# A causal mask added by VectorE in PSUM for short attention jobs, by a TensorE matmul for long ones

## What is computed

```
def masked_softmax(s, mask):
    sf = jnp.where(mask, s.astype(jnp.float32), NEG)      # NEG = -1e30
    m = jnp.max(sf, axis=-1, keepdims=True)
    e = jnp.where(mask, jnp.exp(sf - m), 0.0)
    p = e / jnp.maximum(jnp.sum(e, axis=-1, keepdims=True), TINY)
    return p.astype(s.dtype)
...
s = jnp.einsum('bgrqd,bgkd->bgrqk', qb, kb) * scale       # NSA, causal
s = jnp.einsum('bhqd,bhkd->bhqk', qb, k) * scale          # MLA, causal
...
x = x + merged @ w_out[l]
x = x + jnp.square(jax.nn.relu(hn @ w_up[l])) @ w_down[l]
```

## Time and profile before

| | |
|---|---|
| median of 3 runs | 1598.51 us (1595.76 to 1598.61) |
| profiled execution, its own time | 1601.22 us |
| span of its profile | 1599.4 us |
| granted TensorE clock, mean | 0.989 of full speed |
| PE busy | 1539.1 us, 96% |
| DVE / ACT / POOL busy | 892.5 / 722.9 / 423.1 us |

### The profile page before, as it was taken

One profiled execution on the slowest core, in us unless ns is written; L12 is line 12 of the kernel. 1 busy time (PEld: TensorE's weight loads), 2 busy tenths in 40 slices (PEclk: granted clock), 3 DMA queues, 4 the chain that ended last, 5 costly groups with the idle time before them and its releaser, 6 DMA issues.

```text
span 1599.4 us, 23215 instructions
## 1 busy us (share of the span) xinstructions
PE 1539.1 (96%) x7566; PEld 1269.8 (79%) x7566; DVE 892.5 (56%) x1354; ACT 722.9 (45%) x1315; POOL 423.1 (26%) x442
## 2 busy tenths in 40 slices
PE   6999999899999999999999999999999999999996
PEld 4888788777888888888888777877778888888885
DVE  5765655566754453535566655555575535454455
ACT  5753666774432222222466546767634322222232
POOL 0301566567010010101011025756740201010010
PEclk9999999999999999999999999999999999999998
DMA  4243221114422322322323412211243222323223
GB/s 181 86 145 126 73 68 67 39 67 139 138 93 94 101 95 92 105 92 94 105 80 119 159 65 61 72 67 41 86 165 106 92 93 95 102 92 104 93 92 106
DMA packets 43526, 155.55 MB, mean 97 GB/s; under 512 B 5312, under 2 KB 5312, under 8 KB 43424
## 3 DMA queue, kind: packets, MB, share of 16 engines
q1 hardware_dynamic: 37440, 134.23, 25.3%
q0 software_dynamic: 5408, 17.95, 3.1%
q10 hardware_dynamic: 576, 2.10, 0.3%
HBM read 143.78 MB, written 10.49 MB: 96 GB/s over the span
## 4 chain that ended last, share of the span: by engine, by line
PE 79%; DVE 6%; issue 6%; ACT 5%; POOL 2%; DMA 1%; ACTq 0%; DVEq 0%; POOLq 0%
PE G L1337 13%; PE G L1339 13%; PE G L1338 13%; PE O L1337 8%; PE O L1338 8%; PE O L1339 8%; PE O L1603 3%; PE T L1579 2%; PE S L1562 2%; POOL wsplit L472 2%; PE T L1337 1%; DVE nmx L1103 1%; PE T L1339 1%; PE T L1338 1%; PE O L1412 1%
## 5 line engine op out<-in xcount | busy, mean ns | idle before, releaser
L569 ACT ACTIVATE wsplit<-stage 128x1024 fp32r<-128x1024 f32 x230 | 243.5, 1059 | 617.9 <-PE G L1339 283.4
L891 DVE TENSOR_TENSOR wsplit<-stage,wsplit 128x1024 fp32r<-128x1024 f32 x184 | 266.2, 1447 | 71.0 <-ACT wsplit L569 70.9
L1337 PE MATMUL G<-xg,wsplit 128*128 128x512 f32 x592 | 244.7, 413 | 15.5 <-DVE xg L895 13.6
L562 POOL TENSOR_TENSOR F<-Y 128x512 f32<-128x512 f32 x64 | 68.4, 1069 | 637.3 <-DVE Y L1307 637.3
L1339 PE MATMUL G<-xg,wsplit 128*128 128x512 f32 x592 | 233.0, 394 | 0.0
L1338 PE MATMUL G<-xg,wsplit 128*128 128x512 f32 x592 | 232.4, 392 | 0.0
L1103 DVE TENSOR_REDUCE nmx<-S 128x1 f32<-128x512 f32 x192 | 93.2, 485 | 110.7 <-PE S L1570 109.4
L726 ACT ACTIVATE F<-S,nmx 128x512 f32<-128x512 f32 x192 | 101.3, 527 | 98.5 <-DVE nmx L1103 98.1
L1337 PEld LDWEIGHTS G<-xg,wsplit 128*128 128x128 f32 x592 | 112.9, 191 | 38.4 <-DVE xg L895 16.0
L1339 PEld LDWEIGHTS G<-xg,wsplit 128*128 128x128 f32 x592 | 112.1, 189 | 24.7
L1338 PEld LDWEIGHTS G<-xg,wsplit 128*128 128x128 f32 x592 | 112.6, 190 | 19.9 <-issue 1.0
(11 more groups left out here) (253 smaller groups left out, 3098.8 us busy)
## 6 DMA issues: line engine op xcount, KB each, us to landing
stage<-units SPq DMA_DIRECT2D x230, 512.0 KB, 3.3
stage_n<-units_n SPq DMA_DIRECT2D x22, 512.0 KB, 3.4
gates<-Y POOLq DMA_DIRECT2D x32, 256.0 KB, 2.8
E<-gates POOLq DMA_DIRECT2D x24, 256.0 KB, 3.7
x<-x_in ACTq DMA_DIRECT2D x4, 512.0 KB, 11.3
F<-gates POOLq DMA_DIRECT2D x8, 256.0 KB, 4.8
out<-F SPq DMA_DIRECT2D x6, 256.0 KB, 2.1
rope<-tables POOLq DMA_DIRECT2D x1, 768.0 KB, 9.9
```

Of the source, the lines that this page charges most:

```text
L562: pool.tensor_tensor(F[:, m % 2, :], Y[:, m % 2, :], Y[:, m % 2, :], ALU.mult)\
L569: act.activation(wslot(u)[:, 0, :], staged(u), ACT.Copy).then_inc(s_whin if u in SN else s_whi, 1)
L891: dve.tensor_tensor(wslot(u)[:, 1, :], staged(u), wslot(u)[:, 0, :], ALU.subtract)\
L1337: pe.matmul(dst, a(0), b(0), start=first, stop=False)
```

## The change

`WIDE = 2` is new. For jobs with `qt < WIDE` the scores group on PE ends with the last product matmul, which now carries `stop` and the signal `s_scores`. DVE, once it has seen `s_scores`, adds the mask in place in PSUM to the 128 diagonal columns (one tensor_tensor, fp32 in PSUM plus bf16 in SBUF, result fp32 in PSUM), waits for that result by the chain, and then takes the maximum as before. For the other jobs nothing changes.

```diff
+WIDE = 2
...
                 def max_of(i):
                     w = (JOBS[i][3] + 1) * P
                     dve.wait_ge(s_scores, l * NJ + (i + 1))
+                    if JOBS[i][3] < WIDE:
+                        diagonal = SB[i % 2][:, w - P:w]
+                        chain.mark(dve.tensor_tensor(diagonal, diagonal, causal, ALU.add))
+                        chain.wait()
                     dve.tensor_reduce(nmx[:, i % 4:i % 4 + 1], SB[i % 2][:, 0:w], AX.X, ALU.max, negate=True)\
                         .then_inc(s_max, 1)
...
+                    masked = qt < WIDE
                     if i < NSA_NJ:
                         for c in range(2):
-                            pe.matmul(dst[:, 0:w], QS[:, 2 * t + e, qt * P:w], KN[:, br, t // 2, c, 0:w],
-                                      start=(c == 0), stop=False)
+                            ins = pe.matmul(dst[:, 0:w], QS[:, 2 * t + e, qt * P:w], KN[:, br, t // 2, c, 0:w],
+                                            start=(c == 0), stop=(masked and c == 1))
                     else:
...
-                        three(dst[:, 0:w], lambda c: MQ[:, t % 2, e, c, qt * P:w], lambda c: MK[:, t % 2, e, c, 0:w],
-                              True, False)
-                    pe.matmul(dst[:, qt * P:w], identb, causal, start=False, stop=True).then_inc(s_scores, 1)
+                        ins = three(dst[:, 0:w], lambda c: MQ[:, t % 2, e, c, qt * P:w],
+                                    lambda c: MK[:, t % 2, e, c, 0:w], True, masked)
+                    if not masked:
+                        ins = pe.matmul(dst[:, qt * P:w], identb, causal, start=False, stop=True)
+                    ins.then_inc(s_scores, 1)
```

## The result

The changed kernel takes 1610.7 us in the median of 5 runs (1606.17 to 1612.07), the kernel before 1595.76 us beside it (1595.2 to 1598.61). The ratio is 1.0073, 95% interval [1.0059, 1.0088]: slower by 9.4 to 14.0 us. The two medians are further apart, 14.9 us, because the five times of each kernel fall into two groups (1606.2 and 1610.7 to 1612.1 us; 1595.2 to 1595.8 and 1598.5 to 1598.6 us). The forecast was 1602.0 us, 3.5 us over before, with a range up to 1608, which the result leaves by 2.7 us. The direction holds, and so does the account of full and thin stretches; the size doesn't, and its largest part came by a path that the forecast didn't follow. The profiled execution has a span of 1608.9 us against 1599.4.

The account below looks back on a forecast made before the run. PE bounds full stretches, the DVE and ACT round thin ones. Per layer 3.99 us added less 2.64 saved, +2.7 for two, plus 0.8 chosen: +3.5, median 1598.5 to 1602.0 us, range 1594 to 1608.

Parts of the forecast that it names:

- full and thin stretches: Attention: in full ones PE is full and DVE half empty; in thin ones PE stands still a quarter of the time.
- What bounds the kernel: PE in full stretches; without filling work, the round of maximum, exponential, copy and rest through DVE and ACT.
- the named signs of being wrong: Addition under 0.2 us or over 0.4, full stretches giving 0.2 per mask, or thin stretches not getting longer.
- The fourteen places: Jobs 3, 6, 7, 14, 38, 58, 62, 63, 75, 78, 79, 82, 86, 87: additions cost 3.99 us a layer.
- the choice of 0.40: Jobs 59, 66, 67, 70, a little off the chain where PE waits: 0.8 us added by choice for both layers.
- The price of the addition: On DVE before the maximum: 0.31 us including the wait for its result, bounds 0.21 and 0.45.
- gain from earlier scores: Where DVE waited for scores (jobs 3, 62, 78, 82, 86), they come 0.07 us earlier, so the addition costs 0.24.
- The worth of a mask matmul: On PE at 22 places a layer: 0.12 us each, bounds 0.04 and 0.231, saving 2.64 us a layer.
- The two full stretches: Jobs 18 to 31 and 42 to 55: eight narrow masks each, every stretch forecast to save 0.96 us.
- In full steps all have more than 0.3 us: DVE's queue behind the addition: reciprocals, rest of job i-5 and projection evacuation have time to spare, hiding the addition.
- I count that end as PE's: Behind 370 us the chain runs through POOL's queue; masks of jobs 94, 95 still count as PE savings, 0.12 each.
- PE runs slower after longer waits: Rival, thin stretches: additions of 10, 59, 66, 67, 70, 71, 74 cost 0.31 each, half clock grows; 1607.3 us, chance 0.20.

Follow-up runs that it names:

- experiment 1: Kernel before, with DVE additions replacing mask matmuls only for jobs 18, 19, 22, 23, 26, 27, 42, 43, 46, 47, 50, 51: ratio 0.9997 to before.
- experiment 9: Kernel before, with DVE additions replacing mask matmuls for all jobs 18 to 29 and 42 to 53: 1592.85 us against 1597.34, ratio 0.9970.
- experiment 2: Changed kernel with all mask matmuls kept as well, additions on top for jobs of one or two key tiles: ratio 1.0090 to the kernel before.
- experiment 5: Changed kernel with jobs 78 and 79 back on PE's mask matmul: ratio 1.0050 to the kernel before.
- experiment 3: Kernel before, without mask matmul or addition for jobs of one or two key tiles, leaving out their causal mask: ratio 0.9989.
- experiment 7: Kernel before, with DVE additions replacing mask matmuls for jobs 90, 91, 94 and 95 alone: ratio 1.0001.
- experiment 6: Changed kernel extended to all 192 masks on DVE, no mask matmul (`WIDE = 4`): ratio 1.0109 to the kernel before.

## Why the prediction was right in direction and too low

**What bounds the kernel: right.** Thin and full stretches behave as the profile of before showed. Experiments 1 and 9 gain where PE is full, 2 and 5 lose where it waits for the round, and the average of 96% for PE told neither. What the profile of the changed kernel was to show came as well (additions of 0.294 us for 0.25 to 0.30, waits of 10.5 us for about 10, DVE 27.0 us longer for about 26), and none of the named signs of being wrong did; none of them looked at the clock.

**The fourteen places: right in sum, in part by luck.** Outside jobs 78 to 81, the thin stretches (2 to 7, 14, 38, 58 to 75, 82 to 91) were forecast at 3.48 us a layer with the choice of 0.40, and measured 3.58. The 0.40 chosen for jobs 59, 66, 67 and 70 was mostly not there: 66 to 75 measured 0.33, forecast 0.19 without it. The other places cost 0.36 more than forecast and filled the gap.

**The price of the addition: slightly too low.** 0.33 us against 0.31, inside its bounds. No gain from earlier scores is seen where it was to make 0.24 of 0.31: the pair 62, 63 was forecast at 0.55 and cost 0.60.

**The worth of a mask matmul: too high for the narrow jobs.** Forecast 0.12 us; measured 0.10 in the pairs of experiments 1 and 3, near 0.12 with the wide ones. The smallest scores give least: job 31, of 128 columns, gains 0.08, while jobs 30 and 54, of 256 columns, gave 0.14 and 0.13. The forecast had said that it took the 256-column value for jobs of 128 columns too. The Trainium skill, "TensorE: Matmul & The Clock Gate", section "Back-to-back issue gap", gives about 81 ns for a matmul of 128 columns in a stream of weight loads and matmuls. Here only the masks of the 128-column jobs come that low (0.07 to 0.08 us); the others stay above it.

**The two full stretches: a term mis-sized.** 16 masks were to save 1.92 us a layer and saved 1.21: 0.3 by the price above, and the rest at the pairs 30, 31 and 54, 55. Missing filling work doesn't explain them alone: steps 19 and 43 have none either, and the pairs 18, 19 and 42, 43 gave the most, 0.25 and 0.23. What steps 31 and 55 have besides is the output of a finished head (0.68 us) in DVE's queue, just ahead of the addition; that the two together use up the cover was not tested. "In full steps all have more than 0.3 us" holds for one addition, not there for two.

**Jobs 94, 95 and 11: the sign failed.** The step was "I count that end as PE's". The chain there runs through POOL's queue, and I took POOL's idle time at 391 us as a sign that PE sets it; but the addition of 95 delays the rest of the probabilities that stands behind it in DVE's queue, and PE waits 0.48 us for it. That is 0.74 us a layer off, and job 11 another 0.33, in a stretch that I had followed through the matmul only.

**The clock: half of a rival came true, at another place.** The forecast named "PE runs slower after longer waits", gave it 0.20 together with seven more additions, and looked at 300 to 320 us. Of the seven, job 10 was free alone, and with 66, 67, 70, 71 and 74 moved as well the marks of 65 to 77 rose by 0.33 us, no more than job 75's addition. The half clock came, and it came behind jobs 78 and 79, where before PE waited 1.62 us and kept its full clock. 1.56 us a layer, 3.1 in all, are the largest single miss. The row that would have pointed there was PE's wait of 1.6 us on POOL's split in the kernel before, which the forecast didn't use; it named the reciprocals in DVE's queue but not what stands behind them in POOL's.

The sum of the misses, per layer: 1.56 for the clock, 0.74 for the end, 0.33 for job 11, 0.71 for the full stretches, 0.10 for the rest: 3.44, which is 5.2 less 1.75.

**Jobs 82 to 91.** The marks of 81 to 93 move by 0.80 us with the additions of 82 to 91 all there (experiment 5), and jobs 90 and 91 alone cost nothing (experiment 7). Two waits of PE carry it: one behind jobs 82 and 83 grows from 0.40 to 0.80 us, and this one, in the kernel before and then in that of experiment 5:

```profile
360.85 0.49 PE L1337 MATMUL G<-on,wsplit 128*128 128x512 f32 x1 [0.38 <-POOL wsplit L472]
```

```profile
363.21 0.49 PE L1343 MATMUL G<-on,wsplit 128*128 128x512 f32 x1 [1.13 <-POOL wsplit L474]
```

The scaling that waits for the reciprocals and the split behind it start at 359.90 and 360.69 us in that kernel, the addition of job 90 only at 362.59. So jobs 86 and 87 carry this wait, by the path that was found at 78 and 79 (reciprocals, scaling, split), here without half clock. The forecast had their price, 0.55 us, and not the path.

## What to carry to other kernels

Moving work between engines is decided job by job: the same edit gained about 0.1 us a mask in full steps and lost 0.33 in thin ones, and choosing the places, wide jobs among them, turned 0.7% lost into 0.3% gained. An addition to an engine's queue has to be followed through every queue behind it (here DVE's reciprocal, POOL's scaling, POOL's split, PE), and a little more of a wait of the matmul engine can cost several times its length: here 0.33 us more of it cost 1.92, by the clock. When edits meet in neighbouring steps, their effects, measured one at a time, don't add up.

## What the runs showed of the hardware

These waits and clocks are of one profiled execution of each kernel. PE's wait in the step before job 82 was 1.60 to 1.63 us in eight kernels, two layers each, and in none of these the granted clock fell behind it. In six kernels it was 1.77 to 2.82 us, and in eleven of the twelve places the clock then stood at half (1.2 GHz of 2.4) for 3.4 us; the twelfth, the second layer of experiment 6 with a wait of 2.82 us, kept 1.00. One such stretch (0.17 of the granted clock lost over 10 us, at half of full speed) cost 1.45 to 1.6 us. It also followed when PE had less to do (experiment 3). The wait's length alone doesn't settle it: the longest wait of the first layer, near 309 us, is 2.11 us in the kernel before, with 0.83 of the clock granted over 308 to 318 us, and 2.11 us in the kernel of experiment 9, with 1.00. What else decides is open.

An fp32 tensor_tensor on DVE of 128 columns that reads and writes PSUM (the mask in bf16 in SBUF) takes 299 ns in the median and 294 in the mean, the one that reads PSUM and writes SBUF 269 ns in the mean.

The kernel before took 1595.0 to 1601.5 us in its repetitions beside the experiments. That is why 0.1% is seen here in the marks of the trace and not in the times.
